# A hybrid decoder layer: bias read backwards, gate columns packed, the start and the first head turns reordered

## The reference, cut to what matters

```
h = rmsnorm(x); proj = h @ w_in             # qa ka va | qb kb vb zb | bb ab | two gates of 1024
attention, 8 heads, two score maps of width 64 each:
  logits = q k^T + bias_table[bucket(i - j)], causal; w = softmax_0 - lam * softmax_1; o = w v
delta rule, 8 heads of 128, chunks:
  qb, kb, vb = silu(causal_conv4(...)); beta = sigmoid(bb); g = -exp(a_log) softplus(ab + dt)
  A = I + strict_lower(kk^T * decay); solve A with [v_beta, k_beta e^g]; state goes from chunk to chunk
x += (sigmoid(g0) * (oa @ w_br_a) + sigmoid(g1) * (ob @ w_br_b)) @ w_out
x += (silu(conv3(up_g)) * conv3(up_v)) @ w_down            # after rmsnorm
x += sigmoid(rmsnorm(x) @ w_ple_gate) * (p @ w_ple_proj)
```

## Time and profile before

| | us |
|---|---|
| median of 3 runs (lowest, highest) | 1157.43 (1157.13, 1157.69) |
| the profiled execution | 1157.37 |
| its span, first to last instruction | 1155.6 |
| PE busy | 1121.9 |
| PEld busy | 898.1 |
| DVE busy | 659.6 |
| POOL busy | 640.3 |
| ACT busy | 550.9 |

### The profile page before, as it was taken

How to read it: one execution, slowest core, us unless ns; L and a number is a source line. 1 busy time by engine, 2 the same in 40 slices (tenths; PEclk the granted TensorE clock), 3 DMA queues, 4 the chain that set the end, 5 groups by cost and what they waited for, 6 DMA issues and landing times.

```text
span 1155.6 us, 16770 instructions
## 1 busy us (share of the span) xinstructions
PE 1121.9 (97%) x5498; PEld 898.1 (78%) x5498; DVE 659.6 (57%) x1043; ACT 550.9 (48%) x888; POOL 640.3 (55%) x769
## 2 busy tenths in 40 slices
PE   6999989999999999999999999999999999999998
PEld 4786667777777777667878888888888888888876
DVE  4567977767666776862213324576776515731644
ACT  4584657566565656551322124544444314433542
POOL 6476255646554564645456554576576744573452
PEclk9999999999999999999999999999999999999999
DMA  8255031331404123223223523233333432332223
GB/s 244 69 138 133 17 102 39 82 88 32 103 17 119 36 66 101 73 56 88 77 76 107 182 73 91 85 104 113 100 91 91 120 99 73 109 96 78 77 80 89
DMA packets 196636, 104.36 MB, mean 90 GB/s; under 512 B 3943, under 2 KB 195418, under 8 KB 196570
## 3 DMA queue, kind: packets, MB, share of 16 engines
q1 hardware_dynamic: 196188, 103.39, 32.1%
q10 hardware_dynamic: 381, 0.15, 0.0%
HBM read 101.40 MB, written 2.13 MB: 90 GB/s over the span
## 4 chain that ended last, share of the span: by engine, by line
PE 41%; POOL 25%; issue 23%; DVE 8%; ACT 3%; DMA 1%; POOLq 0%; SPq 0%; DVEq 0%; ACTq 0%
PE bank L567 30%; POOL w_lo L497 25%; PE bank L703 2%; PE bank L717 1%; DVE prod L1818 1%; DVE xs L1820 1%; PE bank L710 1%; PE bank L662 1%; DMA x_tok<-in_x 1%; PE bank L927 1%; DVE pr L1730 1%; DVE oa_lo L1986 0%; PE bank L914 0%; DVE pr L1729 0%; PE bank L924 0%
## 5 line engine op out<-in xcount | busy, mean ns | idle before, releaser
L497 POOL TENSOR_TENSOR w_lo<-w_raw,w_hi 128x256 fp32r<-128x256 f32 x692 | 556.5, 838 | 255.6 <-ACT w_hi L1080 249.8
L567 PE MATMUL bank<-hn_hi,w_hi 128*128 128x512 f32 x1000 | 407.7, 408 | 2.5 <-POOL w_lo L497 1.6
L567 PE MATMUL bank<-hn_hi,w_lo 128*128 128x512 f32 x1000 | 391.0, 391 | 0.0
L567 PE MATMUL bank<-hn_lo,w_hi 128*128 128x512 f32 x1000 | 390.4, 390 | 0.0
L567 PEld LDWEIGHTS bank<-hn_hi,w_hi 128*128 128x128 f32 x1000 | 189.0, 189 | 45.4 <-issue 10.6
L567 PEld LDWEIGHTS bank<-hn_hi,w_lo 128*128 128x128 f32 x1000 | 188.0, 188 | 40.3
L567 PEld LDWEIGHTS bank<-hn_lo,w_hi 128*128 128x128 f32 x1000 | 188.8, 189 | 34.2 <-issue 1.2
L512 POOL CAST w_hi<-w_raw 128x1024 fp32r<-128x1024 f32 x70 | 78.8, 1126 | 216.6 <-PE bank L567 125.6
L1080 ACT ACTIVATE w_hi<-w_raw 128x1024 fp32r<-128x1024 f32 x111 | 117.9, 1062 | 77.7 <-PE bank L567 69.8
L2111 DVE SCALAR_TENSOR_TENSOR u<-vr,pt,u 128x511 f32<-128x511 f32 x88 | 90.5, 1029 | 8.0 <-DVE u L2111 0.2
L567 PE MATMUL bank<-fa_hi,w_hi 128*128 128x512 f32 x176 | 68.5, 389 | 0.0
(11 more groups left out here) (313 smaller groups left out, 1645.0 us busy)
## 6 DMA issues: line engine op xcount, KB each, us to landing
w_raw<-in_w_in SPq DMA_DIRECT2D x73, 512.0 KB, 6.8
w_raw<-in_w_up SPq DMA_DIRECT2D x44, 512.0 KB, 3.7
w_raw<-in_w_down SPq DMA_DIRECT2D x16, 512.0 KB, 3.9
crow<-cum_rows_out SPq DMA_DIRECT2D x16, 256.0 KB, 5.8
w_raw<-in_w_br_a SPq DMA_DIRECT2D x8, 512.0 KB, 3.9
w_raw<-in_w_br_b SPq DMA_DIRECT2D x8, 512.0 KB, 3.9
w_raw<-in_w_out SPq DMA_DIRECT2D x8, 512.0 KB, 4.0
w_raw<-in_w_ple_gate SPq DMA_DIRECT2D x8, 512.0 KB, 4.1
```

What stands on the lines that cost most here:

```text
L497: ins = pool.tensor_tensor(wlo[c.slot][:, ks, :], raw[c.slot][:, ks, :], whi[c.slot][:, ks, :].bitcast(F32), ALU.subtract)
L567: mm = pe.matmul(acc, w[c.slot][:, i, :], xx[:, x0 + i, :], start=(i == 0 and n == 0), stop=last)
```

## The change

The engine orders change as follows.

- *Bias.* The line is stored in reverse order, the skewed read lands directly in `bias`, and `maxima` reads `bias` with a negative step. The `slope` tile, the matrix `flip`, its products and the copies are gone. The load is issued behind the keys' loads; the line's product stands behind the turned gates.
- *Gate columns.* Only 16 columns are loaded. GpSimd lays their high and low parts side by side in 32 columns of `w_hi`, and `gate_products` takes two products a step, interleaved with the first key's gemm. The two parts are added in the product that turns the gates, with the constant `pick` in place of a transpose.
- *First key.* Its convolution stands on VectorE ahead of the chain of the gates.
- *Start.* The squares of tile 1 are made on VectorE, tiles 1 and 2 share one root chain, the constants are loaded after tile 1, the parameters are copied before the last tile, `sums_r` is cast after the low halves. TensorE runs five products of zeros at the start and a sixth between the transposes.
- *Lead and turn 0.* `scores` and `maxima` come ahead of substitution steps, and 11 of the steps move into turn 0. Turning back, pairing and placing move later; the mask of the first `dec` goes to GpSimd, which waits for `turned_back` at its fourth chunk of turn 0 in place of its first.
- *Halves.* `halves(g)` alternates the low products of group g + 1 with the high ones of group g, in one place of a turn; turn 0 has `halves(-1)` and `halves(0)`. ScalarE's copies move with them.
- *Norms.* `first_two` puts a step of the second gemm ahead of the first's last, the last two `gather` follow the last low half, and ScalarE makes one high part of the last stage ahead of the norm's root.

The core of the diff:

```diff
 STEPS = ((2, 3, 1, 8, 1, 8, 1, 9), ((1, 1), (1, 1, 1), (1, 1, 1), (1, 1, 1)))
-STEPS_FIRST = ((2, 4, 1, 9, 1, 8, 1, 8), ((1, 1), (1, 1, 1), (1, 1, 1), (1, 1, 1)))
+STEPS_FIRST = ((2, 4, 1, 10, 1, 8, 1, 8), ((1, 1), (1, 1, 1), (1, 1, 1), (1, 1, 1)))
...
-    r = 255 - np.arange(LINE)
+    r = 255 - np.arange(LINE)[::-1]
...
+    c[:, C_PICK:C_HOT] = np.arange(P)[:, None] % 16 == np.arange(16)[None, :]
...
-                if t == 0:
-                    sp.dma_start(sq[:, :], consts[:, 0:C_HOT * P]).then_inc(sem("consts_in"), 16)
-            load(stream.ba.at(0), w_in0, COLS["ba"])
...
+                if t == 1:
+                    sp.dma_start(sq[:, :], consts[:, 0:C_HOT]).then_inc(sem("consts_in"), 16)
+            gate_cols = w_in0[:, COLS["ba"]:COLS["ba"] + 16].rearrange("(k p) n -> p k n", p=P)
+            sp.dma_start(raw[0][:, :, 0:16], gate_cols).then_inc(arrived[0], 16)
+            load(stream.keys.at(0), w_in0, COLS["kb"])
...
-            sp.wait_ge(sem("line_out"), 16)
-            skew = bass.AP(tensor=dram_line.tensor, offset=0, ap=[[1, P], [LINE, H], [1, 256]])
-            sp.dma_start(slope[:, :, :], skew).then_inc(sem("slope_in"), 16)
-            for n in (3, 4):
-                load(stream.keys.at(n), w_in0, COLS["kb"] + n * P)
...
+            sp.wait_ge(sem("line_out"), 16)
+            skew = bass.AP(tensor=dram_line.tensor, offset=1, ap=[[1, P], [LINE, H], [1, 256]])
+            sp.dma_start(bias[:, :, :], skew).then_inc(sem("bias_in"), 16)
...
-            for c in [stream.ba.at(0)] + [stream.keys.at(n) for n in range(H)]:
-                both(c)
+            pool.wait_ge(arrived[0], 16)
+            pool.tensor_copy(whi[0][:, :, 0:16], raw[0][:, :, 0:16]).then_inc(high_ready, 1)
+            pool.wait_ge(high_ready, 1)
+            pool.tensor_tensor(whi[0][:, :, 16:32], raw[0][:, :, 0:16], whi[0][:, :, 0:16].bitcast(F32),
+                               ALU.subtract).then_inc(low_ready, 1)
+            for n in range(H):
+                both(stream.keys.at(n))
...
+            pool.wait_ge(sem("dec"), 1)
+            pool.tensor_tensor(dec[:, :, :], dec[:, :, :], cum.unsqueeze(1).to_broadcast([P, NT, P]),
+                               ALU.mult).then_inc(sem("dec_cut"), 1)
...
-                    if h == 0 and n == 0:
+                    if h == 0 and n == 3:
...
+            def idle_product():
+
+                pe.matmul(bank[1][:, :], wT[:, 0, 0:P], wT[:, 0, :], start=True, stop=True)
+
+            pe.wait_ge(sem("eps_set"), 5)
+            for n in range(5):
+                idle_product()
...
-            pe.wait_ge(sem("lines_in"), 16 * 2)
-            pe.wait_ge(sem("eps_set"), 4)
-            pe.matmul(bank[6][0:H, 0:LINE], tab[:, :], hot[:, :], start=True, stop=True).then_inc(sem("line_mm"), 1)
+            idle_product()
...
-            run(gemm(stream.ba.at(0), hn_hi, hn_lo, ready=("h_split", 0)))
-            f = Fill(*[gemm(stream.keys.at(n), hn_hi, hn_lo) for n in range(H)],
+            def gate_products(i):
+
+                pe.wait_ge(low_ready, 1)
+                pe.wait_ge(sem("h_split"), i + 1)
+                for n, xx in enumerate((hn_hi, hn_lo)):
+                    mm = pe.matmul(bank[0][0:32, :], whi[0][:, i, 0:32], xx[:, i, :],
+                                   start=(i == 0 and n == 0), stop=(i == KD - 1 and n == 1))
+                if i == KD - 1:
+                    mm.then_inc(product_ready, 1)
+
+            f = Fill(gemm(stream.keys.at(0), hn_hi, hn_lo, ready=("h_split", 0)))
+            for i in range(3):
+                gate_products(i)
+            for i in range(KD):
+                f.step(1)
+                if i + 3 < KD:
+                    gate_products(i + 3)
+            f = Fill(*[gemm(stream.keys.at(n), hn_hi, hn_lo) for n in range(1, H)],
                      *[gemm(stream.first.at(n), hn_hi, hn_lo) for n in range(len(FIRST))])
             f.step(2)
...
-                mm = pe.transpose(bank[5][:, t * 16:t * 16 + 16], ba_sb[:, t * P:(t + 1) * P], ident[0:16, 0:16])
+                mm = pe.matmul(bank[5][:, t * 16:t * 16 + 16], ba_sb[:, t * P:(t + 1) * P], pick[0:32, :], start=True, stop=True)
             mm.then_inc(sem("ba_T"), 1)
-            f.step(6)
+            pe.wait_ge(sem("lines_in"), 16 * 2)
+            pe.wait_ge(sem("eps_set"), 4)
+            pe.matmul(bank[6][0:H, 0:LINE], tab[:, :], hot[:, :], start=True, stop=True).then_inc(sem("line_mm"), 1)
+            f.step(5)
...
-            f.step(2)
-            pe.wait_ge(sem("slope_in"), 16)
-            pe.wait_ge(sem("line_ready"), 1)
-            for n in range(H // 2):
-                if n >= 2:
-                    pe.wait_ge(sem("bias_ready"), n - 1)
-                pe.matmul(bank[6 + n % 2][:, :], flip, slope[:, 2 * n:2 * n + 2, :].rearrange("p a b -> p (a b)"),
-                          start=True, stop=True).then_inc(sem("bias_mm"), 1)
-            f.step(4)
+            f.step(1)
...
+            def halves(g):
+
+                pe.wait_ge(sem("placed"), 2 if g < 0 else 6)
+                pe.wait_ge(sem("pairs"), 1 if g < 1 else 2)
+                if g >= 0:
+                    pe.wait_ge(sem("inverse_ui"), g + 3)
                 if g > 0:
                     pe.wait_ge(sem("ob_sum_read"), g)
                 for n in range(8):
+                    if g < H // 2 - 1:
+                        low = low_half(8 * g + 8 + n)
+                    if g >= 0:
+                        high = high_half(8 * g + n)
+                if g < H // 2 - 1:
+                    low.then_inc(sem("inverse_u"), 1)
+                if g >= 0:
+                    high.then_inc(sem("inverse_x"), 1)
...
+                if h == 0:
+                    f.step(7)
+                    pair_low(0)
+                    f.step(1)
+                    pair_low(1)
+                    f.step(before[3] - 8)
+                    turn_w(a, 1)
+                    f.step(before[4])
...
+                if 0 < h < H // 2:
+                    halves(h)
...
-                run(gemm(c, hn_hi, hn_lo, ready=("n_split", stage * KD)))
+                one = Fill(gemm(c, hn_hi, hn_lo, ready=("n_split", stage * KD)))
                 f = Fill(gemm(then, x_hi, x_lo, k))
-                f.step(2)
+                one.step(KD - 1)
+                f.step(1)
...
+            for n, (t, t0) in enumerate(((0, 0), (2, 1), (3, 3))):
+                if t == 2:
+                    act.wait_ge(sem("x_sq"), 1)
+                these = slice(t0, t + 1)
+                link(nc.scalar.activation(lnx[:, these], ss0[:, these], ACT.Ln, bias=sm[:, 28:29], scale=1.0 / D))
+                done(nc.scalar.activation(rs0[:, these], lnx[:, these], ACT.Exp, scale=-0.5), "x_r", n + 1)
...
+                if stage == 1:
+                    high(stream.ple.at(3))
...
+            dve.wait_ge(sem("x_in1"), 16)
+            done(V.scalar_tensor_tensor(out=junk1[:, :], in0=x_tok[:, 1, :], scalar=1.0, in1=x_tok[:, 1, :],
+                                        op0=ALU.mult, op1=ALU.mult, accum_out=ss0[:, 1:2]), "x_sq", 1)
...
-                return bias[:, bass.ds(h, 1), 256 - near:256].rearrange("p a b -> p (a b)")
+                return bias[:, bass.ds(h, 1), near - 1::-1].rearrange("p a b -> p (a b)")
...
+                if h == 0:
+                    maxima(a, 0)
+                    substitute(20, 21)
+                    combine(a, 0)
+                    substitute(21, 31)
+                    turn_back()
+                    maxima(a, 1)
+                    turn_again()
+                    combine(a, 1)
+                    scaled_keys()
+                    scaled_values()
...
             def lead_turn(at):
 
-                prep(0, 1)
-                substitute(0, 3)
                 maxima(0, 0)
-                substitute(3, 5)
+                substitute(0, 2)
                 combine(0, 0)
-                substitute(5, 8)
+                substitute(2, 4)
                 maxima(0, 1)
-                substitute(8, 10)
+                substitute(4, 6)
                 combine(0, 1)
                 steps(conv(0, 0, at("qb")))
                 maxima(0, 2)
-                substitute(10, 12)
+                substitute(6, 8)
                 combine(0, 2)
                 steps(conv(0, 2, at("vb")))
                 maxima(0, 3)
                 steps(finish_silu(0, 0))
-                substitute(12, 13)
+                substitute(8, 9)
                 combine(0, 3)
-                substitute(13, 18)
+                substitute(9, 14)
                 prep(1, 0)
-                substitute(18, 24)
+                substitute(14, 20)
+                attention_scale(0)
+                prep(1, 1)
                 steps(finish_silu(0, 2))
-                attention_scale(0)
-                substitute(24, 28)
-                first_mask()
-                prep(1, 1)
-                substitute(28, 31)
-                turn_back()
...
+            c = stream.ba.at(0)
```

(87 more changed lines are left out.)

245 lines of the change are left out of this document (121 added, 124 removed).

## The result

The changed kernel takes 1160.24 us (median of 20 runs, 1157.87 to 1162.22), the kernel before 1157.45 beside it: a ratio of 1.0022, 95% interval 1.0016 to 1.0029. It is 2.8 us slower where 14.5 us less were forecast, outside the range. Its profiled execution took 1159.33 us, with a span of 1157.4 (1155.6 before).

A forecast was written before the change was run, and what follows sets the result against it. TensorE was taken to run products end to end with few waits, following ScalarE and VectorE at the start. A 5.4, B 2.5, C 1.6, D 3.8 and E 1.2 sum to 14.5 off 1157.37: 1142.9 us, range 1138.5 to 1149.5.

The forecast's parts named there:

- A: Launch to the end of the first key's gemm: ends at 27.0 in place of 32.4, a gain of 5.4 us.
- B: The gates' stage: four flips go, less new products and a 0.9 us wait, a gain of 2.5 us.
- that rival: Start: the clock falls back between first products and gates, A gains only 2.4, time 1145.9 us; chance 0.22.
- C: Lead and turn 0: old waits go, new ones come, a gain of 1.6 us, bounds -3 and +4.8.
- the old waits: Lead and turn 0: TensorE's waits from substitution steps ahead of `combine`, 6.9 us taken off in C.
- The substitution's part: Turn 0: GpSimd's splits lengthen VectorE's substitution by 4.5 us, 0 to 9.6; full cost gives 1147.5, chance 0.12.
- D: Turns 1 to 3: alternated half products overlap and save 1.28 us a turn, a gain of 3.8 us.
- E: The tail: an earlier ScalarE copy shortens TensorE's 1.57 us wait for a split, a gain of 1.2 us.
- The slower rival: `maxima`: the reversed bias read takes k times as long, eating the gain at k = 2.1; chance 0.04.

The follow-up runs named there:

- e_before_pad16: The kernel before with 16 unused columns behind its constants, so its later tiles begin 64 bytes past a multiple of 256: 1160.12 us.
- e_no_warm: The changed kernel without its six products of zeros, with 48 unused columns behind its constants: 1159.34 us.
- e_pool_first: The changed kernel with GpSimd's stop after the first chunk of turn 0 in place of the fourth: 1166.67 us.
- e_turn0_new: The best kernel with the changed order of turn 0 on TensorE, ScalarE and VectorE: 1156.00 us.
- e_idle: The changed kernel with four unread products on TensorE, two ahead of turn 0's first scores and two ahead of its first pair products: 1159.72 us.
- e_pool_second: The changed kernel with GpSimd's stop after the second chunk of turn 0 in place of the fourth, and 48 unused columns: 1156.77 us.
- e_layout: The changed kernel with 112 unused columns behind its constants, so every later tile has its address of the kernel before: 1157.46 us.
- the best kernel: The changed kernel with the order of the kernel before in lead and turn 0 on four engines, and 48 unused columns: 1149.92 us.

## Why the prediction was wrong

**A and B held in mechanism; that their sum came out exactly is luck.** Forecast 7.9 us together, measured 7.9. The first high half came at 14.05 (forecast 15.0), the gate products at 16.86 (17.9), the first key's gemm ended at 26.2 (27.0). So A gave 6.3 us where 5.4 were forecast. B gave 1.6 where 2.5 were: at the cumulative sums TensorE waited 0.1 us, not 0.9, but I had added up durations that overlap. From start to start the four flips took 3.8 us (35.82 to 39.64), not 4.4, and the picking products took 1.0 us where the transposes took 0.35. One execution is also no exact measure of a start: counted from `e_before_pad16`, A and B give 6.7 us. The clock stayed up through the transposes: that rival did not come true, and `e_no_warm` gives the warming its size.

**C is the step that failed.** It was put at a gain of 1.6 us, bounds -3 and +4.8, and was a loss of 9.9 (8.7 counted from `e_before_pad16`). Of the 9.9, 3.7 are idle time of TensorE and 6.2 busy time. The sum also took off all 6.9 us of the old waits, though it gave a reason for 4.8 only; the old wait at turn 0's first turning (2.1) did go. The substitution's part was about right: it took 6.0 us more of VectorE (31.0, 25.0 before), where I charged 4.5 and allowed up to 9.6, and `pair_low` waited 2.5 us (forecast 3.3). Wrong were three things.
- I charged waits in too few places. The first scores of turn 0 wait 2.6 us (I took 0.5), the third scores 1.8 and the lead 1.7 (I took none), the last turning 2.4 (I took 1.5). I had the slow substitution steps hold up `pair_low` alone, but the key's preparation for turn 0's first scores stands behind nine operations of 0.8 to 1.4 us (0.42 undisturbed) in VectorE's queue: with GpSimd stopped earlier (`e_pool_first`) that wait is 0.8. `e_turn0_new` shows that turn 0's order costs 6.1 us even with the substitution done in time: a wait that small products used to cover is as much a cost as a new one.
- The clock fell behind waits. I had looked at the clock only at the start. In turn 0 it was at the lower level for 13.7 us (granted clock 0.90 of 68.69 us), and busy time grew by 6.1 us. That the waits cause the falls is shown for one only: `e_idle` filled it and the fall went. The profiled execution of the kernel before also had a higher clock than its others (0.999 over the whole, mostly 0.995 to 0.998 elsewhere, where the changed kernel has 0.992 to 0.996), so the usual difference in busy time is smaller.
- GpSimd's stop had two prices. Behind the fourth chunk it lengthens the substitution; ahead of it TensorE lacks a chunk (14.8 us in `e_pool_first`, 4.2 in `e_pool_second`). Of the orders tried, stop and substitution fit only with the old lead.

**D was mis-sized.** The halves overlap as forecast (turns 2 and 3 gain 1.3 us each), but turn 1 gains 0.1, with waits of 0.54 and 0.34 us that it did not have. 2.6 us, not 3.8. **E held**: 1.2 us, the wait of 1.57 became 0.38.

**A term was missing.** Taking the flip out of `sq` moved every later tile. I took that edit for free. It costs 2.65 us, shown from both sides (`e_layout`, `e_before_pad16`), and is the size of the whole difference between the two kernels. Without it the forecast would still have missed the profiled execution by 13.8 us, 11.5 of them in C.

**The slower rival was the wrong one.** The backward read costs nothing; `maxima`'s subtraction over the whole kernel, after (ns min/median/max):

```profile
L1748 DVE TENSOR_TENSOR bank<-bank,bias x64: 287/423/433, 96.4 to 485.1; 128x256 f32<-128x256 f32 x48, 128x128 f32<-128x128 f32 x16
```

In the kernel before the median is 423 too. My 0.04 for slower stood on this alone, and my bounds of C left out what I had not priced.

Left open: 0.6 us between 509 and 515, in some kernels with either order of turn 0; why 128 bytes cost more than 64; why some waits of 2.4 us are followed by a fall of the clock and others not; and which of turn 0's moves is worth what, since the moves of TensorE, ScalarE and VectorE were only tried together. The gain of the best kernel over before (7.5 us) is less than A, B, D and E sum to (11.7), since its lead has waits of 2.8 and 1.5 us and the clock falls in it as well (0.96 and 0.97).

## What to carry to other kernels

An engine's small work ahead of a wait is cover: before moving it, ask what the engine will do in that time, and what its clock will do. When an edit changes a tile's size, check where every later tile then begins. When a change has many parts, take the parts one by one: here start, halves and tail were gains, and the reordering between them gave all of it back.

## What the hardware showed

- **Address of the moving operand.** 48 products of 512 columns take 10.88 us when the tiles begin at a multiple of 256 bytes, 11.00 when 64 past it (two kernels), 11.19 when 128 past it (one kernel). Over the late stage that is 0, 2.65 and 6.6 us. It is the moving operand that counts: 384 products in a row whose moving operand is `hn_hi` or `hn_lo`, tiles that did not move, take 87.2 us in both kernels.
- **GpSimd beside VectorE.** One step of the substitution with 256 elements takes 0.42 us alone. Beside GpSimd's mask and cast, and then its split, after:

```profile
129.94 0.42 DVE L1854 TENSOR_TENSOR prod<-li,xs 128x256 f32<-128x256 f32 x1
130.40 1.40 DVE L1856 TENSOR_TENSOR xs<-xs,prod 128x256 f32<-128x256 f32 x1
131.83 1.14 DVE L1854 TENSOR_TENSOR prod<-li,xs 128x255 f32<-128x255 f32 x1
133.01 0.85 DVE L1856 TENSOR_TENSOR xs<-xs,prod 128x255 f32<-128x255 f32 x1
...
130.08 1.44 POOL L530 TENSOR_TENSOR dec<-dec,sq 128x512 f32<-128x512 f32 x1 [19.29 <-ACT dec L1361]
131.46 1.24 POOL L515 CAST w_hi<-w_raw 128x1024 fp32r<-128x1024 f32 x1
132.77 2.54 POOL L500 TENSOR_TENSOR w_lo<-w_raw,w_hi 128x256 fp32r<-128x256 f32 x3
```

The step of 130.40 ends at 131.80, 0.3 us behind the mask; the next ends 0.3 us behind the cast, and the one under the split takes twice the time. The Trainium skill (SBUF — State Buffer, SBUF: two separate sides) describes the pair of ports that VectorE and GpSimd share as a lock that is held for a whole instruction; the rows agree.
- **The clock in mid-kernel.** It fell to half after waits of 1.8 to 2.6 us, at different places in each kernel, and the best kernel has such falls as well (0.95 in the window at 100 us, 0.66 in that at 155). Waits of 2.46 and 2.37 us elsewhere were followed by none.
